# Keeping one block's outputs on chip instead of two, reading the last token rows behind the other block's scatter, and summing nine read pairs on TensorE over eight banks

## The chip, the cores and the metric

One core of one Trainium2 chip runs the whole program in one launch. The metric is the device time of an execution in microseconds (us). The kernel before takes 1036.44 us, the median of 3 runs (1035.94 to 1037.66).

## The reference

One layer of a hybrid backbone works on 640 tokens (128 prompt, 512 latent) of width 1024: a modulated norm, one input projection, a Fourier mixer and windowed attention, an output projection, then a mixture of experts and a last norm. The change lies in the mixture of experts and in the last norm behind it, and these lines say what they compute:

```python
idx, gates = route(xf, w_router, router_bias)          # 8 of 64 experts per token
...
def expert_block(args):
    tok, e = args
    xb = xpad[tok]
    hb = jax.nn.silu(xb @ w_gate[e]) * (xb @ w_up[e])
    return hb @ w_down[e]
rows = lax.map(expert_block, ...)
routed = jax.ops.segment_sum(rows.reshape(R, D) * row_gate[:, None], row_tok, ...)[:N]
shared = (jax.nn.silu(xf @ ws_gate) * (xf @ ws_up)) @ ws_down
...
x = x + gate * (routed + shared)
y = rms_norm(x, norm_f)
```

Everything is float32. Each token gets the gated outputs of eight experts summed; the eight are called its picks.

## The kernel before, in words

Tokens stand in five tiles of 128 (T = 5; tile 0 is the prompt). The routed rows are sorted into 49 blocks (NQ = 49, numbered 0 to 48) of four groups of 32 rows, each group with one expert. For each block GpSimd gathers 128 token rows, TensorE transposes them (`x_in`), multiplies with the gate and up weights (`block_gate_up`, 64 instructions), ScalarE and VectorE form silu(gate) * up (`silu`, `gated`), TensorE transposes that (`block_h`), and multiplies with the down weights (`block_down`, 32 instructions). ScalarE and VectorE scale half of the result each by the routing gate into `yb` (`y_half`, `y_out`), and GpSimd scatters the rows into a table in HBM, `expert_rows` (`y_dram`), by indirect DMA (line 791). Rows that hold no token are not written. The expert weights come through SP's queue into five homes (`ring` and a part of `reg_p`), 3 MB for an expert, each load issued when the home's former expert has been used.

The table has for each token tile eight picks of 128 rows. The picks of a token are sorted by expert. At the end SP reads the table back (line 706) in 20 requests of 1 MB, one for each token tile t and pair of picks j (`REQUESTS`, `PART = (6, 4, 2, 0)`: j = 0 are picks 6 and 7, j = 3 are picks 0 and 1). Request n goes into buffer n for the first 12, then buffers 5 to 11 are used again, each when its former content has been summed (`freed`). All go through one queue. The picks with high numbers can't come from the last experts, so request 0 needs block 44 scattered, and request 5 block 46.

The last two blocks, 47 (`KEPT`) and 48, are not scattered at all in the kernel before. Their rows in the table are set to zero early on (two indirect DMAs of zeros, line 824), and their outputs stay in `yb`. One-hot matrices `token_hit` (VectorE, `kept_tokens`) let TensorE add them to each tile's sum: out = token_hit x yb, two per block and tile (line 2320, line 2335 for the last tile). A read pair is summed in one of two ways: by VectorE with two additions of 128x1024 (`more_rows`, lines 1671 and 1672), or by TensorE with four products with the identity into the same banks (line 2327, line 2342). `PE_PAIRS` says which. j = 0 is always summed by VectorE within itself (`first_rows`, line 1666). `joined(t)` adds TensorE's sum to VectorE's, times the modulation gate, to the token tile `xs` (lines 1680, 1683, 1685), ScalarE then squares and roots (lines 1179, 1182), `finished(t)` scales by the norm (lines 1660, 1661), and SP writes the tile out (line 714). The last tile is done in two column halves (lines 1718, 1719, 1727; SP line 718). A float32 product of 128x512 stands in the trace as two MATMUL records.

## Time and profile before

| what | value |
|---|---|
| median of 3 runs | 1036.44 us |
| the profiled execution, its own time | 1036.7 us |
| its span in the trace | 1034.9 us |
| TensorE busy share of the span | 96% |
| VectorE | 33% |
| ScalarE, GpSimd | 22%, 16% |
| from HBM and to HBM | 298.76 MB, 31.39 MB |
| granted TensorE clock, mean | 0.992 |

The shares are means over stages with different limits. The blocks run from about 389 us to 985 us; the stage that the change rewrites is the last 70 us. A view with a time window shows which engine is full there and what another one waits for.

### The profile page before, as it was taken

The page shows a single profiled execution, that of the slowest core. Times are in us where ns is not written, and L with a number is a line of the kernel's source. Part 1 is how long each engine was busy: PE and PEld are TensorE (multiplying, and loading weights), DVE is VectorE, ACT ScalarE, POOL GpSimd, SP SyncE. Part 2 cuts the span into 40 slices and gives each one's busy share as a digit, 9 for nine tenths or more (in the row PEclk, how much of TensorE's full clock was granted, in tenths as well). Part 3 has the DMA queues.
Part 4 walks back from the last instruction along what each step waited for, and adds up shares of the span by engine and source line. Part 5 has one row for each costly group of instructions (what it writes and reads, how often), then busy time and mean ns, then how long its engine had stood idle before and what let it go on. Part 6 is the DMA issues. An engine that isn't in the chain of part 4 may idle for free.

```text
span 1034.9 us, 17713 instructions
## 1 busy us (share of the span) xinstructions
PE 997.8 (96%) x7069; PEld 445.8 (43%) x7069; DVE 338.3 (33%) x857; ACT 230.2 (22%) x549; POOL 161.9 (16%) x233
## 2 busy tenths in 40 slices
PE   6999999999999999999999999999999999999896
PEld 4435556565455553444333333333334433433242
DVE  1022225765136772322111111111112111112398
ACT  2131105665122240112111111111112111112111
POOL 1000010300131022111212211111211222111000
PEclk9999999999999999999999999999999999999998
DMA  9985408400101199999999999999999999999993
GB/s 326 384 333 192 163 32 226 201 2 1 62 21 41 48 387 388 398 421 420 419 422 421 417 420 380 400 421 419 419 419 419 414 372 399 419 420 420 419 409 139
DMA packets 64562, 321.60 MB, mean 311 GB/s; under 512 B 9768, under 2 KB 18624, under 8 KB 35040
## 3 DMA queue, kind: packets, MB, share of 16 engines
q1 hardware_dynamic: 48064, 272.71, 65.8%
q0 software_dynamic: 14240, 43.34, 10.6%
q10 hardware_dynamic: 2176, 4.41, 1.2%
q8 instruction: 57, 0.93, 0.4%
q14 instruction: 25, 0.20, 0.1%
HBM read 298.76 MB, written 31.39 MB: 319 GB/s over the span
## 4 chain that ended last, share of the span: by engine, by line
PE 83%; DMA 8%; DVE 5%; ACT 2%; issue 1%; SPq 1%; POOL 0%; DVEq 0%; POOLq 0%; ACTq 0%
PE bank L2211 30%; PE bank L2231 15%; PE bank L1973 7%; PE bank L1772 6%; DMA ring<-in_w_up 4%; PE bank L1756 4%; PE bank L2183 4%; PE bank L2067 3%; PE bank L2000 2%; PE bank L1986 2%; PE bank L1821 1%; PE bank L2073 1%; DMA ring<-expert_rows 1%; PE bank L1957 1%; DMA ring<-in_w_mod 1%
## 5 line engine op out<-in xcount | busy, mean ns | idle before, releaser
L2211 PE MATMUL bank<-ring,reg_h 128*32 128x512 f32 x2512 | 341.5, 598 | 5.3 <-DMA ring<-in_w_up 5.3
L2211 PEld LDWEIGHTS bank<-ring,reg_h 128*32 128x32 f32 x2512 | 102.4, 111 | 193.5 <-issue 193.3
L2231 PE MATMUL bank<-ring,reg_y 128*32 128x512 f32 x1256 | 174.1, 594 | 2.8 <-ACT reg_y L1109 2.0
L2211 PE MATMUL bank<-reg_p,reg_h 128*32 128x512 f32 x624 | 126.7, 592 | 0.0
L1597 DVE TENSOR_TENSOR reg_h<-reg_p,bank 128x256 f32<-128x256 f32 x49 | 20.6, 421 | 312.3 <-ACT reg_p L1127 282.1
L1127 ACT ACTIVATE reg_p<-bank 128x256 f32<-128x256 f32 x49 | 18.8, 384 | 309.0 <-PE bank L2211 309.0
L791 POOL DMA_INDIRECT expert_rows<-reg_y,rowc x47 | 47.3, 1007 | 239.3 <-DVE reg_y L1582 228.9
L2231 PEld LDWEIGHTS bank<-ring,reg_y 128*32 128x32 f32 x1256 | 48.0, 110 | 84.6 <-issue 79.6
L1582 DVE TENSOR_SCALAR reg_y<-bank,reg_p 128x512 f32<-128x512 f32 x49 | 36.8, 751 | 130.6 <-PE bank L2231 130.6
L1973 PE MATMUL bank<-ring,reg_h 128*128 128x512 f32 x160 | 70.3, 594 | 0.0
L1116 ACT ACTIVATE reg_y<-bank,reg_p 128x512 f32<-128x512 f32 x49 | 33.7, 688 | 151.0 <-PE bank L2231 147.3
L2231 PE MATMUL bank<-reg_p,reg_y 128*32 128x512 f32 x312 | 65.1, 593 | 0.0
L1772 PE MATMUL bank<-ring,reg_h 128*128 128x384 f32 (+2 forms) x192 | 63.2, 487 | 0.0
L777 POOL DMA_INDIRECT reg_h<-h_rows,tokc x49 | 51.3, 1047 | 39.2 <-POOL tokc L806 20.1
L2211 PEld LDWEIGHTS bank<-reg_p,reg_h 128*32 128x32 f32 x624 | 34.3, 110 | 42.6 <-issue 42.6
L2183 PE MATMUL bank<-keep,reg_h 128*128 128x128 f32 x392 | 48.5, 276 | 0.1
L2183 PEld LDWEIGHTS bank<-keep,reg_h 128*128 128x128 f32 x392 | 46.0, 192 | 2.8 <-issue 1.7
L1772 PEld LDWEIGHTS bank<-ring,reg_h 128*128 128x128 f32 x192 | 36.0, 190 | 25.7 <-issue 12.6
L1973 PEld LDWEIGHTS bank<-ring,reg_h 128*128 128x128 f32 x160 | 29.8, 190 | 34.6 <-issue 34.6
L1756 PE MATMUL bank<-ring,reg_h 128*128 128x512 f32 x96 | 43.0, 596 | 1.5 <-ACT reg_h L901 1.5
L1571 DVE COPY reg_h<-bank 128x512 f32<-128x512 f32 x49 | 33.9, 691 | 19.3 <-PE bank L2183 19.2
L1360 DVE CUSTOM_DVE_ANT_0 ring<-bank,reg_b,nsink 128x512 f32<-128x512 f32 (+2 forms) x60 | 34.5, 614 | 11.2 <-PE bank L1957 11.1
(304 smaller groups left out, 988.6 us busy)
## 6 DMA issues: line engine op xcount, KB each, us to landing
ring<-in_w_gate SPq DMA_DIRECT2D x51, 1024.0 KB, 13.2
ring<-in_w_up SPq DMA_DIRECT2D x51, 1024.0 KB, 19.9
ring<-in_w_down SPq DMA_DIRECT2D x51, 1024.0 KB, 17.5
ring<-in_w_mod SPq DMA_DIRECT2D x20, 1024.0 KB, 6.7
ring<-expert_rows SPq DMA_DIRECT2D x19, 1024.0 KB, 13.5
reg_p<-in_w_gate SPq DMA_DIRECT2D x13, 1024.0 KB, 16.6
reg_p<-in_w_up SPq DMA_DIRECT2D x13, 1024.0 KB, 21.8
reg_p<-in_w_down SPq DMA_DIRECT2D x13, 1024.0 KB, 19.8
```

The costliest lines, as they stand in the source:

```text
L777: pool.indirect_dma_start(out=xg[:, p, :], out_offset=None, in_=h2_dram, in_offset=bass.IndirectOffsetOnAxis(ap=tokc[:, p:p + 1], axis=0), ...
L791: pool.indirect_dma_start(out=y_dram, out_offset=bass.IndirectOffsetOnAxis(ap=rowc[:, p:p + 1], axis=0), in_=yb[:, p, :], in_offset=None, ...
L1116: act.activation(yb[:, p, 0:512], bank[source][:, :], ACT.Copy, scale=gate).then_inc(s_ya, 1)
L1360: dve.tensor_tensor_reduce(prob[:, p % 3, b, 0:nk], bank[2 * (p % 2) + b][:, 0:nk], masks[:, m0:m0 + len(keys), :].rearrange("p a b -> p ( ...
L1571: dve.tensor_copy(xg_t[:, p, 512:1024], source[:, :]).then_inc(s_xb, 1)
L1582: dve.tensor_scalar(yb[:, p, 512:1024], bank[source][:, :], gate, None, ALU.mult).then_inc(s_yb, 1)
L1756: last = pe.matmul(bank[2 + 3 * t + g][:, :], h1t[:, k, t * P:(t + 1) * P], w[:, 512 * g:512 * g + 512], start=(k == 0), stop=(k == KD - 1))
L1772: last = pe.matmul(bank[4 + g % 2][:, 0:WIDTHS[g]], h1t[:, k, t * P:(t + 1) * P], win_part(k, g), start=(k == 0), stop=(k == KD - 1))
L1973: last = pe.matmul(bank[2 * (t % 2) + hf][:, :], mix_t[:, k, t * P:(t + 1) * P], w, start=(k == 0), stop=(k == KD - 1))
L2183: last = pe.transpose(bank[banks[k // 4]][:, (k % 4) * P:(k % 4 + 1) * P], v[:, k, :], ident)
L2211: last = pe.matmul(bank[2 + p][R * j:R * j + R, :], xg_t[:, p, k * P + R * j:k * P + R * j + R], w_gu(homes[n % SLOTS])[:, k], start=(k == ...
L2231: last = pe.matmul(bank[y_banks(b)[hf]][R * j:R * j + R, :], h_t[:, p, i * P + R * j:i * P + R * j + R], w_dn(homes[n % SLOTS])[:, i, 512 ...
```

## The change

Block 47's outputs are no longer kept. GpSimd scatters them behind all the other scatters (a new indirect DMA with its own row numbers `rowk`), and only block 48 keeps zeros in the table, one-hots and products. Requests 10 to 19 hold all picks 0 to 3 and wait for that scatter. To have block 47's outputs early, its down product is put between the two halves of block 48's gate and up products, and ScalarE writes both halves of them. The order of reads changes from tile by tile to all j = 0, all j = 1, then j = 2 and 3 tile by tile. TensorE sums nine pairs instead of seven, each of the first four tiles in two banks of its own, and VectorE sums six instead of eight.

```diff
-        PE_PAIRS = ((3,), (3,), (3,), (2, 3), (2, 3))
+        PE_PAIRS = ((3,), (2, 3), (2, 3), (2, 3), (2, 3))
-            return t if j == 0 else ACC + 3 * t + j - 1
+            return t + ACC * j if j < 2 else 2 * ACC + 2 * t + j - 2
...
-            sp.wait_ge(s_zero, 32)
+            sp.wait_ge(s_zero, 16)
             for n, (t, j) in enumerate(REQUESTS):
...
+                if n == 2 * ACC:
+                    sp.wait_ge(s_zero, 32)
...
-            for p in range(2):
-                pool.indirect_dma_start(out=y_dram, out_offset=bass.IndirectOffsetOnAxis(ap=rowc[:, p:p + 1], axis=0),
-                                        in_=zeros, in_offset=None,
-                                        bounds_check=NROW - 1, oob_is_err=False).then_inc(s_zero, 16)
+            pool.indirect_dma_start(out=y_dram, out_offset=bass.IndirectOffsetOnAxis(ap=rowc[:, 0:1], axis=0),
+                                    in_=zeros, in_offset=None,
+                                    bounds_check=NROW - 1, oob_is_err=False).then_inc(s_zero, 16)
...
+            pool.wait_ge(s_ya, KEPT + 1)
+            pool.wait_ge(s_yb, KEPT + 1)
+            pool.indirect_dma_start(out=y_dram, out_offset=bass.IndirectOffsetOnAxis(ap=rowk[:, 0:1], axis=0),
+                                    in_=yb[:, KEPT % 2, :], in_offset=None,
+                                    bounds_check=NROW - 1, oob_is_err=False).then_inc(s_zero, 16)
...
             silu(KEPT, 1)
-            silu(KEPT + 1, 0)
             h_t_out(KEPT, 1)
             y_half(KEPT, 1, extra * 16 + scattered(KEPT), gate_s[:, KEPT:KEPT + 1], y_banks(KEPT)[0])
+            act.activation(yb[:, 1, 512:1024], bank[y_banks(KEPT)[1]][:, :], ACT.Copy, scale=gate_s[:, KEPT:KEPT + 1]).then_inc(s_yb, 1)
+            silu(KEPT + 1, 0)
...
             block_gate_up(KEPT)
-            block_gate_up(KEPT + 1)
+            block_gate_up(KEPT + 1, range(KD // 2))
             block_h(KEPT, 1)
             block_down(KEPT)
+            block_gate_up(KEPT + 1, range(KD // 2, KD))
             block_h(KEPT + 1, 0)
             block_down(KEPT + 1)
...
-            for t in range(T - 2):
+            gated(KEPT, 1)
+            for t in range(4):
                 first_rows(t)
-            gated(KEPT, 1)
-            first_rows(T - 2)
             gated(KEPT + 1, 0)
-            first_rows(T - 1)
-            y_half(KEPT, 1, extra * 16 + scattered(KEPT), gate_s[:, KEPT:KEPT + 1], y_banks(KEPT)[1])
+            first_rows(4)
             more_rows(0, 1)
             y_out(KEPT + 1)
+            for t in range(1, T):
+                more_rows(t, 1)
             more_rows(0, 2)
...
```

On TensorE, at the head of the tail in the kernel before, behind block 48's down product (line 2320 adds kept rows with one-hots in `reg_b`, line 2327 adds read rows in `ring`; a row is one product, which the trace shows as two records):

```order
L2320 MATMUL bank0<-reg_y,reg_b 128x512
L2320 MATMUL bank1<-reg_y,reg_b 128x512
...
L2327 MATMUL bank0<-ring,keep 128x512
L2327 MATMUL bank1<-ring,keep 128x512
...
L2320 MATMUL bank2<-reg_y,reg_b 128x512
L2320 MATMUL bank3<-reg_y,reg_b 128x512
...
L2327 MATMUL bank2<-ring,keep 128x512
L2327 MATMUL bank3<-ring,keep 128x512
```

And in the changed kernel at the same place (its lines 2318 and 2326 are those of 2320 and 2327 before):

```order
L2318 MATMUL bank0<-reg_y,reg_b 128x512
L2318 MATMUL bank1<-reg_y,reg_b 128x512
L2318 MATMUL bank2<-reg_y,reg_b 128x512
L2318 MATMUL bank3<-reg_y,reg_b 128x512
L2318 MATMUL bank4<-reg_y,reg_b 128x512
L2318 MATMUL bank5<-reg_y,reg_b 128x512
L2318 MATMUL bank6<-reg_y,reg_b 128x512
L2318 MATMUL bank7<-reg_y,reg_b 128x512
L2326 MATMUL bank0<-ring,keep 128x512
L2326 MATMUL bank1<-ring,keep 128x512
```

Before, each tile had four products with kept rows and then four or eight with read rows, over banks 0 to 3 in turn. Now eight products with kept rows of four tiles stand first, 28 with read rows of those tiles follow with nothing between them, and the last tile has one kept and four read products for each of its two halves.

On TensorE, where blocks 47 and 48 are multiplied, before (line 2211 gate and up, 2073 transposes, 2231 down; bank3 is block 47's, bank2 block 48's):

```order
L2211 MATMUL bank3<-ring,reg_h 32x512 x32
L2211 MATMUL bank2<-ring,reg_h 32x512
L2211 MATMUL bank2<-reg_p,reg_h 32x512 x3
...
L2073 MATMUL bank4<-keep,reg_h 128x128 x2
L2231 MATMUL bank0<-ring,reg_y 32x512 x8
```

And in the changed kernel (lines 2213, 2074, 2234):

```order
L2213 MATMUL bank2<-reg_p,reg_h 32x512 x3
L2074 MATMUL bank4<-keep,reg_h 128x128 x2
L2234 MATMUL bank0<-ring,reg_y 32x512 x8
L2234 MATMUL bank1<-ring,reg_y 32x512 x8
L2213 MATMUL bank2<-ring,reg_h 32x512
```

Block 47's transposes and its down product moved ahead of half of block 48's gate and up products.

On SP, the reads of the table before, the last rows of the queue (the names in brackets are the semaphores that a read waits for):

```order
L706 DMA ring<-expert_rows 128x2048 [waits block_gate_up_done] x4
L706 DMA ring<-expert_rows 128x2048 [waits block_down_done] x2
L706 DMA ring<-expert_rows 128x2048 [waits second_rows_summed_by_dve] x2
L706 DMA ring<-expert_rows 128x2048 [waits token_rows_summed_by_pe]
```

And in the changed kernel:

```order
L710 DMA ring<-expert_rows 128x2048 [waits block_gate_up_done] x4
L710 DMA ring<-expert_rows 128x2048 [waits block_down_done,zero_rows_then_last_but_one_block_out]
L710 DMA ring<-expert_rows 128x2048 [waits block_down_done]
L710 DMA ring<-expert_rows 128x2048 [waits second_rows_summed_by_dve] x6
L710 DMA ring<-expert_rows 128x2048 [waits token_rows_summed_by_pe]
```

Request 10, the second of these rows, now waits for the scatter of block 47, and six reads instead of five wait for VectorE's sums.

## Rows read from the trace of the kernel before

**Rows 1.** The page: busy time of an engine; DMA share in 40 slices of the span

```profile
PE 997.8 (96%) x7069; PEld 445.8 (43%) x7069; DVE 338.3 (33%) x857; ACT 230.2 (22%) x549; POOL 161.9 (16%) x233
...
DMA  9985408400101199999999999999999999999993
```

**Rows 2.** The chain that ended last, from 930 us: start, us, what

```profile
1025.76 1.28 DVE xs L1661
...
1028.37 0.61 DVE reg_h L1718
```

**Rows 3.** Timeline of TensorE in the tail: start, us, instruction, count, [idle before]

```profile
985.14 3.70 PE L2320 MATMUL bank<-reg_y,reg_b 128*128 128x512 f32 x8
...
1009.28 7.03 PE L2327 MATMUL bank<-ring,keep 128*128 128x512 f32 x16
1016.14 1.88 PE L2335 MATMUL bank<-reg_y,reg_b 128*128 128x512 f32 x4
...
1023.01 3.60 PE L2342 MATMUL bank<-ring,keep 128*128 128x512 f32 x8
```

**Rows 4.** Timeline of VectorE and SP's queue in the tail

```profile
988.89 1.23 DVE L1671 TENSOR_TENSOR ring<-ring 128x1024 f32<-128x1024 f32 x1 [0.42 <-DMA ring<-expert_rows]
...
993.93 1.28 DVE L1680 TENSOR_TENSOR ring<-ring,bank 128x512 f32<-128x512 f32 x2
...
997.65 1.22 DVE L1671 TENSOR_TENSOR ring<-ring 128x1024 f32<-128x1024 f32 x1
...
1016.10 0.34 SPq L714 DMA_DIRECT2D out_y_prompt<-xs  x1
```

**Rows 5.** Timeline of all engines around blocks 47 and 48

```profile
960.57 0.75 DVE L1582 TENSOR_SCALAR reg_y<-bank,reg_p 128x512 f32<-128x512 f32 x1 [3.73 <-PE bank L2231]
962.17 0.97 POOL L791 DMA_INDIRECT expert_rows<-reg_y,rowc  x1 [4.52 <-DVE reg_y L1582]
...
967.43 0.38 ACT L1127 ACTIVATE reg_p<-bank 128x256 f32<-128x256 f32 x1 [6.18 <-PE bank L2211]
...
968.82 1.23 DVE L1666 TENSOR_TENSOR ring<-ring 128x1024 f32<-128x1024 f32 x1 [7.50 <-DMA ring<-expert_rows]
...
975.75 0.51 PE L2073 MATMUL bank<-keep,reg_h 128*128 128x128 f32 x2 [1.51 <-DVE reg_h L1597]
...
980.57 0.69 ACT L1116 ACTIVATE reg_y<-bank,reg_p 128x512 f32<-128x512 f32 x1 [3.90 <-PE bank L2231]
```

**Rows 6.** SP's queue, 969 to 972 us, and all DMAs on the table, issue to landing

```profile
970.12 2.18 SPq L706 DMA_DIRECT2D ring<-expert_rows  x3
...
DMA to landing us min/median/max: 8.2/10.3/20.1
```

**Rows 7.** GpSimd's zero scatters, and DMA queues from 414.9 to 422 us

```profile
410.55 0.99 POOL L824 DMA_INDIRECT expert_rows<-reg_b,rowc  x1 [0.30 <-issue]
...
q0 software_dynamic: 272, 0.62, 22.2%
```

**Rows 8.** Timeline of TensorE at its two waits for weights

```profile
530.45 5.77 PE L2211 MATMUL bank<-ring,reg_h 128*32 128x512 f32 x36 [2.06 <-DMA ring<-in_w_up]
...
674.81 5.43 PE L2211 MATMUL bank<-ring,reg_h 128*32 128x512 f32 x36 [3.25 <-DMA ring<-in_w_up]
```

**Rows 9.** Stretches: us, busy us (instructions) by engine, granted clock, DMA share, GB/s

```profile
530.84:534.24 3.40, 3.40 (x20) 1.08 (x16) 0.00 (x0) 0.00 (x0) 0.23 (x1) 0.50 1.02 425
534.25:540.00 5.75, 5.75 (x55) 2.41 (x48) 0.30 (x1) 0.69 (x2) 0.00 (x0) 1.00 1.01 422
674.20:677.60 3.40, 2.79 (x16) 0.92 (x20) 0.00 (x0) 0.00 (x0) 0.05 (x1) 0.50 1.00 418
677.70:682.00 4.30, 4.30 (x44) 1.36 (x40) 0.00 (x0) 0.00 (x0) 0.00 (x0) 1.00 1.02 424
...
985.14:1026.61 41.47, 41.47 (x100) 18.15 (x96) 39.93 (x41) 7.75 (x14) 0.00 (x0) 1.00 0.72 296
```

**Rows 10.** A stretch while the weights stream, columns as above

```profile
600.00:640.00 40.00, 40.00 (x368) 16.05 (x364) 7.84 (x19) 7.54 (x15) 8.78 (x15) 1.00 0.96 395
```

More of the change, by code:

```diff
@@ L1602, in kept_tokens @@
             def kept_tokens():
-                dve.wait_ge(s_zero, 32)
-                for i in range(2):
-                    kept = slice(KEPT + i, KEPT + i + 1)
-                    for t in range(T):
-                        last = dve.tensor_scalar(token_at[:, i, t:t + 1], tok_i[:, kept], float(-t * P), None, ALU.add)
+                dve.wait_ge(s_zero, 16)
+                for t in range(T):
+                    last = dve.tensor_scalar(token_at[:, t:t + 1], tok_i[:, KEPT + 1:KEPT + 2], float(-t * P), None, ALU.add)
                 link(last)
-                for i in range(2):
-                    for t in range(T):
-                        last = dve.tensor_scalar(token_hit[i][:, t, :], iota, token_at[:, i, t:t + 1], None, ALU.is_equal)
+                for t in range(T):
+                    last = dve.tensor_scalar(token_hit[:, t, :], iota, token_at[:, t:t + 1], None, ALU.is_equal)
                 last.then_inc(s_kept, 1)
@@ L1679, in joined @@
                     cols = slice(512 * hf, 512 * hf + 512)
-                    last = dve.tensor_tensor(half[:, cols], half[:, cols], bank[2 * (t % 2) + hf][:, :], ALU.add)
+                    last = dve.tensor_tensor(half[:, cols], half[:, cols], bank[2 * t + hf][:, :], ALU.add)
                 last.then_inc(s_tq, 1)
@@ L1713, in _ @@
             link(dve.tensor_tensor(xs[:, t, :], xs[:, t, :], ahead, ALU.add))
+            joined(1)
+            finished(0)
+            joined(2)
+            finished(1)
+            joined(3)
+            finished(2)
             finished(T - 2)
@@ L2309, in _ @@
             pe.wait_ge(s_kept, 1)
-            pe.wait_ge(s_ya, KEPT + 1)
-            pe.wait_ge(s_yb, KEPT + 1)
+            pe.wait_ge(s_ya, NQ)
+            pe.wait_ge(s_yb, NQ)
             for t in range(T - 1):
-                if t >= 2:
-                    pe.wait_ge(s_tq, t - 1)
-                for i, p in ((0, 1), (1, 0)):
-                    if t == 0 and i:
-                        pe.wait_ge(s_ya, NQ)
-                        pe.wait_ge(s_yb, NQ)
-                    for hf in range(2):
-                        pe.matmul(bank[2 * (t % 2) + hf][:, :], token_hit[i][:, t, :], yb[:, p, 512 * hf:512 * hf + 512],
-                                  start=(i == 0), stop=False)
+                for hf in range(2):
+                    pe.matmul(bank[2 * t + hf][:, :], token_hit[:, t, :], yb[:, (KEPT + 1) % 2, 512 * hf:512 * hf + 512],
+                              start=True, stop=False)
+            for t in range(T - 1):
                 for j in PE_PAIRS[t]:
```

59 lines of the change are left out of this document (25 added, 34 removed).

## The prediction

> **What bounds the kernel now.** I read the page first, then the chain of waits of the last 100 us, then the timeline there engine by engine, and then stretches of it. The page says that TensorE is busy 96% of the span and that the DMA engines are full from slice 17 on, with a thin last slice [rows 1]. So two things are full at once in the expert stage, and it takes the rows to see which one ends last where.
>
> In the tail the chain runs over VectorE: from the addition at 988.89 us, over the scaling at 1025.76, to the last half's product at 1028.37 nearly every link is a VectorE instruction [rows 2, 4]. The reader should see that this is close. From 985.14 to 1026.61 us TensorE is busy for all of 41.47 us and VectorE for 39.93 us [rows 9]. TensorE's rows follow each other without idle time: 16 records from 1009.28 to 1016.14, that is 0.429 us each, and 0.858 us for a product of two [rows 3]. It ends at 1023.01 + 3.60 = 1026.61, and VectorE comes to the last half's bank only at 1028.37 [rows 2, 3].
>
> The third player is the stream of reads. The ninth read (request 8) releases VectorE at 988.89; the last one releases SP's first output at 1016.10 [rows 4]. That is 11 reads in 27.21 us, 2.47 us for a read of 1 MB. All before them were queued as closely. So the k-th read lands at 988.89 + 2.47 (k - 9), and the twelfth (request 11) at 996.3. Before the change this pace hurts nobody, since VectorE and TensorE both get work from the reads in step.
>
> **The change part by part.**
>
> *Fewer products and additions.* TensorE had 5 x 4 products with kept rows and 7 x 4 with reads, 48 in all. It gets 5 x 2 and 9 x 4, 46: 1.7 us less work. VectorE loses two pairs, each two additions of 1.25 us (988.89 to 997.65 holds four of these and the joining of tile 0; the joining takes 997.65 - 993.93 = 3.72), so 5.0 us of work less [rows 4]. If work were all, the tail would be shorter.
>
> *The new order of reads.* Requests 0 to 10 are now all VectorE's, and 11 to 19 are all TensorE's. TensorE's products with kept rows can start when block 48's output is there. After that it has nothing until request 11 lands. Where is it by then? Block 48's gate and up products start when block 47's silu starts, at 967.43 [rows 5], and take 6.9 us; the first half ends at 970.85. Block 47's transposes follow at once, because `gated` now stands ahead of `first_rows` on VectorE; before, they waited until 975.75 [rows 5]. From transposes to the scaled output it takes 980.57 - 975.75 = 4.8 us [rows 5], so ScalarE starts on block 47's output at 975.7 and, with two activations of 0.69 us [rows 5], is through at 977.1. Block 48's second half runs 975.3 to 978.7, its silu and `gated` take about 1.1 us, and its output is ready at 979.8 + 4.8 + 0.7 = 985.3. That is where the kernel before started its products with kept rows (985.14 [rows 3]), so nothing is lost or won. Eight products take 6.9 us: TensorE runs dry at 992.2.
>
> *The scatter of block 47.* Between the end of the scaling (961.32) and the issue (962.17) there were 0.85 us before [rows 5], so it is issued at about 977.9. The last scatter before was issued at 962.17 and let SP go on at 970.12, 7.95 us later; over all DMAs on this table the figures are 8.2, 10.3 and 20.1 us [rows 5, 6]. So it lands at about 986 (985.9 to 998). Request 10 waits for it. But the reads ahead of it last until 991.4 in the pace above, so SP's wait is covered by what is queued: the read has to be issued some 1.4 us before the queue runs empty. The cover is gone if the scatter takes over 13 us. Behind request 10 in SP's queue stand the other nine reads; their buffers are free in time (VectorE ends a pair each 2.5 us from 984 on). The scatter's own bytes do cost: at most 128 rows of 4 KB, 0.52 MB or 1.24 us at 422 GB/s [rows 9]; the two zero scatters of blocks 47 and 48 are most of 0.62 MB on the software queue, so 0.31 MB or 0.73 us each if equal [rows 7]. I take **+1.0 us** on every later read (0.73 to 1.24). Request 11 then lands at 997.3.
>
> *TensorE behind it.* From there on TensorE needs 0.858 x 4 = 3.43 us for a pair and a pair lands each 2.47 us, so it is never short again, and never has a pause either. Seven pairs, then one kept product and two pairs in two halves: 28 + 2 + 8 = 38 products, 32.6 us. With 0.3 us to start it ends at 1030.2, and VectorE comes to the last half at 1030.4 instead of 1028.37: **+2.0 us**. VectorE is not later than that by itself: tile 3 can be joined at 997.6 + 7 x 3.43 = 1021.6, then 3.7 for joining, twice 1.5 for the scaling of tiles 2 and 3 (an instruction of 1.28 [rows 2] behind a reciprocal), and 1.4 for the first half: 1029.7, 0.7 us ahead. What follows it to the end is unchanged.
>
> *The clock.* TensorE stands still from 992.2 to 997.6, 5.4 us. In the trace a pause of 2.06 us is followed by a stretch with a granted clock of 0.50 (1.2 instead of 2.4 GHz), and so is one of 3.25 us [rows 8, 9], while the pause of 1.51 us at 975.75 isn't [rows 5, 9]. The new pause is longer than both, so I expect one such stretch. Its price: 20 instructions in 3.40 us where 55 in 5.75 us is the pace after it (12.5 instructions or 1.3 us lost), and 16 in 2.79 us against 44 in 4.30 us (1.2 us lost) [rows 9]; halved throughout it would be 1.7. For these dense products I take **+1.5 us**, with 0 and two stretches, 3.0, as bounds.
>
> *The zero scatter that goes.* It saves GpSimd 0.99 us, hidden, and the DMA engines its bytes, 0.73 to 1.24 us, at a place from which they are full (share 1.01 at 422 GB/s) [rows 7, 9]. TensorE waits twice for weights, 2.06 and 3.25 us [rows 8]. Both landings move forward: **-1.0 us** for everything after 674.81. More is possible: a pause of 1.06 us may leave the clock up at 530.84 and save another 1.3 us, which lasts only if the loads around 600 to 640, where DMA is not quite full (0.96), follow TensorE [rows 9, 10]. Less too, if homes and not bytes set these landings. Bounds 0 and -2.3. The shorter one-hot work on VectorE is beside block products and costs or gives nothing.
>
> *Sum.* 1036.7 (the profiled execution) - 1.0 + 2.0 + 1.5 = 1039.2. The median of the runs is 0.3 us below that execution, so 1038.9.
>
> **The rivals.**
>
> *Smaller than can be told.* The same tail, with the weights' landings 2.3 us earlier: 1036.4 - 2.3 + 2.0 + 1.5 = 1037.6. Or with no low clock: 1036.4 - 1.0 + 2.0 = 1037.4. For it: half of the terms are single pauses. Against it: the pause is 5.4 us.
>
> *Faster: VectorE was the bound and is relieved.* If TensorE were never without reads, its 46 products would run from 985.3 to 1024.8 and VectorE would come to the last half at 1025.0, 3.4 us earlier; with the zero scatter's 1.0 us that is 1032.0. The chain of waits speaks for it, as it names VectorE at almost every step [rows 2]. It decides from the point where request 11 lands by 992.2; the pace of the reads puts that 5 us later, and no part of the change moves bytes away from before it.
>
> *Slower still: a late scatter.* If block 47's scatter lands later than about 991, each further us is a us at the end. With the longest, 20.1 us, it lands at 998, the end moves by 7 us to 1045.9. The scatter before was issued while VectorE had nothing to do for 7.50 us; the new one falls among additions of 1.23 us with both inputs in SBUF [rows 5]. Four of them in its way would be 5 us, and it would land at 991, at the edge. The Trainium skill, page "SBUF — State Buffer", section "Who interferes with whom", has such a rule: a VectorE instruction with two SBUF inputs contends with a GpSimd instruction that reads SBUF. By that rule the scatter's issue is held up by VectorE; no row of this trace shows a scatter beside such additions, so it is open here.
>
> **How the numbers follow.** The forecast (pause on TensorE, low clock, weights about 1 us earlier) 0.56; smaller than can be told 0.28; relieved and faster 0.06; late scatter 0.06; something else 0.04, split. 0.2% is 2.07 us, about what a measurement of this kernel can tell from no change. The forecast itself goes from 1038.0 to 1040.7, and a part of it lies within 0.2%: slower 0.58, same 0.34, faster 0.08. The range has to take in the smaller cases, down to 1036.6 (all of -2.3 and no full stretch of low clock), and up to 1041.0 (no gain from the weights, more than one stretch).
>
> **What would show it.** In the changed kernel's timeline TensorE has, behind the kept products (line 2318), a pause of about 5 us that a DMA on `expert_rows` ends at about 997, then 76 records without a gap, and a stretch with clock 0.50 at or just behind the pause. VectorE, full before, has idle time in front of `joined` (line 1687), ended by TensorE. SP's request 10 is issued at about 986 and the reads keep their 2.47 us. The last halves (line 1719) wait for TensorE. The pause at 530 is about 1 us. I am wrong if TensorE's first read pair starts before 994, if the reads' stream has a hole behind the scatter, or if the end waits for VectorE.

## The result, and the profile after

The changed kernel takes 1041.83 us, the median of 8 runs (1039.36 to 1044.12), against 1036.19 us for the kernel before (8 runs, 1033.97 to 1039.55). The ratio is 1.0048, with a 95% interval of 1.0032 to 1.0064: 5 us slower. That is the direction of the forecast, but above its 1038.9 us and above the upper end of its range, 1041.0.

The page of the changed kernel answers to [rows 1]. TensorE is as busy as before, VectorE has 6.6 us less work, and the DMA line is nearly the same.

```profile
PE 998.0 (96%) x7065; PEld 445.6 (43%) x7065; DVE 331.7 (32%) x842; ACT 230.9 (22%) x550; POOL 162.5 (16%) x233
...
DMA  9994409300110199999999999999999999999993
```

The chain that ended last no longer runs over VectorE, as it did in [rows 2]. From 970 us on it is (start, us, what):

```profile
975.91 9.95 DMA expert_rows<-reg_y,rowk
...
985.88 0.32 SPq L710
...
986.24 9.53 DMA ring<-expert_rows
...
995.81 26.50 PE bank L2326 x56
1022.31 0.86 PE bank L2333 x2
1023.17 3.43 PE bank L2340 x8
1026.61 0.86 PE bank L2333 x2
1027.46 3.45 PE bank L2340 x8
...
1030.93 0.70 DVE reg_h L1719
```

Read it from the bottom: the last half of the last tile waits for TensorE, TensorE has worked without a break since 995.81, it started there because a read of the table landed, and the chain goes on through SP's queue to the scatter of block 47. The timelines of TensorE and VectorE show the same from their side:

```profile
983.71 7.11 PE L2318 MATMUL bank<-reg_y,reg_b 128*128 128x512 f32 x16 [1.07 <-DVE reg_y L1592]
995.81 26.50 PE L2326 MATMUL bank<-ring,keep 128*128 128x512 f32 x56 [5.00 <-DMA ring<-expert_rows]
...
1001.82 1.28 DVE L1687 TENSOR_TENSOR ring<-ring,bank 128x512 f32<-128x512 f32 x2 [5.64 <-PE bank L2326]
...
1030.93 0.69 DVE L1719 TENSOR_TENSOR reg_h<-bank,reg_b 128x512 f32<-128x512 f32 x1 [0.43 <-PE bank L2340]
```

Both engines stand still, TensorE for 5.00 us and VectorE for 5.64. Three stretches (columns as in [rows 9]) add the clock:

```profile
983.71:995.81 12.10, 7.11 (x16) 2.93 (x16) 11.64 (x10) 0.00 (x0) 0.00 (x0) 0.90 0.90 359
995.81:1000.28 4.47, 4.47 (x6) 1.89 (x7) 0.37 (x1) 0.00 (x0) 0.00 (x0) 0.50 1.02 429
1000.28:1030.90 30.62, 30.62 (x72) 13.29 (x70) 24.11 (x28) 7.42 (x14) 0.00 (x0) 1.00 0.58 236
```

Behind the pause the granted clock is 0.50 for 4.47 us, in which 6 records get done; at full clock each takes 0.43 us. The clock had already fallen inside the pause:

```profile
993.45:1000.28 6.83, 4.47 (x6) 1.89 (x7) 2.66 (x3) 0.00 (x0) 0.00 (x0) 0.50 1.02 428
```

The half clock lasts 6.83 us, and TensorE works for 4.47 of them. The read that it waits for lands 9.53 us behind its request, and from 1000.28 on the DMA share is only 0.58: all reads are early except the one that TensorE starts with.

**A fixed point to measure from.** Executions differ in their first 76 to 79 us, so two traces are compared by the distance to a fixed point P, the start of the eight small transposes that follow TensorE's wait of 0.94 us there (line 1788; line 1787 before). In the changed kernel:

```profile
76.22 1.06 PE L1788 MATMUL bank<-keep,ring 128*128 128x128 f32 x8 [0.94 <-DVE ring L1269]
```

In the kernel before the row starts at 78.10. From P to the end of the span it is 1034.9 - 78.10 = 956.8 us before and 1037.5 - 76.22 = 961.3 after: 4.5 us. The medians differ by 5.6 us, the own times of the two profiled executions only by 2.7 (1039.36 - 1036.7), since that of the changed kernel is the shortest of its eight and has its P 1.9 us earlier. P moves with the clock at the very start. From 14 to 18 us (first the kernel before, then the changed one):

```profile
14.00:18.00 4.00, 3.04 (x16) 0.68 (x16) 0.00 (x0) 0.00 (x0) 0.00 (x0) 0.68 1.01 391
14.00:18.00 4.00, 3.40 (x28) 1.81 (x29) 0.88 (x2) 0.00 (x0) 0.00 (x0) 1.00 1.02 387
```

Over all 17 traces of this document, the nine whose P is at 77.78 us or later have a clock of 0.83 from 10 to 20 us, and the eight whose P is at 76.95 or earlier have 1.00, whichever kernel it is.

### The profile page after: what moved, and what is told of

It is laid out like the page before. It is cut to its first block, busy times and chain, and to the rows that moved or that the text cites. A ratio compares the mean times of both kernels' runs of the same rounds, so it can differ in the third digit from the quotient of the medians.

```text
span 1037.5 us, 17689 instructions
## 1 busy us (share of the span) xinstructions
PE 998.0 (96%) x7065; PEld 445.6 (43%) x7065; DVE 331.7 (32%) x842; ACT 230.9 (22%) x550; POOL 162.5 (16%) x233
## 4 chain that ended last, share of the span: by engine, by line
PE 87%; DMA 7%; DVE 2%; ACT 1%; issue 1%; SPq 1%; DVEq 0%; POOLq 0%; ACTq 0%
PE bank L2213 30%; PE bank L2234 15%; PE bank L1974 7%; PE bank L1773 6%; DMA ring<-in_w_up 4%; PE bank L1757 4%; PE bank L2184 4%; PE bank L2068 3%; PE bank L2326 3%; PE bank L2001 2%; PE bank L2081 2%; PE bank L2074 2%; PE bank L1987 2%; PE bank L1822 1%; PE bank L1958 1%
## 5 line engine op out<-in xcount | busy, mean ns | idle before, releaser
L795 POOL DMA_INDIRECT expert_rows<-reg_y,rowc x47 | 47.4, 1010 | 239.1 <-DVE reg_y L1592 237.7
L781 POOL DMA_INDIRECT reg_h<-h_rows,tokc x49 | 51.2, 1045 | 39.0 <-POOL tokc L810 20.8
```

Of the source, the lines that this page charges most:

```text
L781: pool.indirect_dma_start(out=xg[:, p, :], out_offset=None, in_=h2_dram, in_offset=bass.IndirectOffsetOnAxis(ap=tokc[:, p:p + 1], axis=0), ...
L795: pool.indirect_dma_start(out=y_dram, out_offset=bass.IndirectOffsetOnAxis(ap=rowc[:, p:p + 1], axis=0), in_=yb[:, p, :], in_offset=None, ...
```

## The experiments

Each was timed beside the kernel before on the same chip, and "before" is the median of that kernel there. "P to end" is from each one's profile, a single execution. Theory A is that of the prediction (standstill, half clock, and reads that come late for TensorE), theory B a late scatter.

| run | us, median | before, beside it | ratio, 95% interval | P | P to end |
|---|---|---|---|---|---|
| (before, profiled) | | | | 78.10 | 956.8 |
| again: the changed kernel | 1041.9 | 1037.4 | 1.0045 (1.0029 to 1.0061) | 76.95 | 962.6 |
| fill | 1039.66 | 1037.4 | 1.0020 (1.0006 to 1.0033) | 76.75 | 959.6 |
| noscatter | 1039.5 | 1037.4 | 1.0019 (1.0002 to 1.0036) | 78.24 | 959.3 |
| fed | 1039.46 | 1037.4 | 1.0013 (0.9997 to 1.0030) | 78.83 | 958.2 |
| split | 1035.91 | 1036.87 | 0.9991 (0.9978 to 1.0003) | 77.78 | 955.7 |
| twozero | 1040.19 | 1036.87 | 1.0034 (1.0019 to 1.0049) | 76.45 | 960.6 |
| relief | 1036.25 | 1036.87 | 0.9998 (0.9983 to 1.0012) | 76.56 | 957.8 |
| offload | 1039.34 | 1036.87 | 1.0028 (1.0014 to 1.0042) | 78.15 | 960.0 |
| fillns | 1038.07 | 1036.27 | 1.0021 (1.0009 to 1.0034) | 76.52 | 958.9 |
| join | 1035.9 | 1036.27 | 1.0002 (0.9987 to 1.0017) | 77.79 | 957.2 |
| splitjoin | 1036.07 | 1036.27 | 0.9996 (0.9983 to 1.0009) | 76.57 | 955.7 |
| warm | 1034.09 | 1036.27 | 0.9981 (0.9968 to 0.9993) | 76.41 | 955.2 |
| warmb | 1037.17 | 1036.9 | 1.0000 (0.9989 to 1.0011) | 77.89 | 958.6 |
| warma | 1039.32 | 1036.9 | 1.0039 (1.0024 to 1.0054) | 78.17 | 959.2 |
| warm2 | 1034.13 | 1036.9 | 0.9975 (0.9964 to 0.9985) | 78.62 | 955.1 |

**again**, the changed kernel without an edit.

> The changed kernel once more, unchanged, for another trace and the clock of each run. Theory A (TensorE is left without reads and then loses clock): a pause of 4.5 to 5.5 us ahead of the first read product, at least 3.4 us of half clock behind it, about 5 us slower than before, and runs with a lower mean clock take longer. Theory B (the scatter of block 47 lands late in most executions and holds the reads): the slower the run, the longer from the scatter's issue to its landing, with a hole in the DMA stream, and no relation to the clock.

It repeats the loss. TensorE and the clock in its trace:

```profile
985.57 7.10 PE L2318 MATMUL bank<-reg_y,reg_b 128*128 128x512 f32 x16 [1.03 <-DVE reg_y L1592]
997.06 7.48 PE L2326 MATMUL bank<-ring,keep 128*128 128x512 f32 x10 [4.38 <-DMA ring<-expert_rows]
```

```profile
997.06:1002.98 5.92, 5.92 (x7) 2.53 (x8) 0.84 (x1) 0.00 (x0) 0.00 (x0) 0.50 1.00 418
```

The pause is shorter than in the first trace (4.38 against 5.00 us), and more of TensorE's work falls under the low clock (5.92 against 4.47 us). Theory B fails on its own sign: from the scatter's issue to SP's next read it is 8.45 us here and 9.95 in the first trace, and this execution is the longer one (1041.33 against 1039.36 us). Theory A's last sign holds only roughly: the shortest four of the twelve runs have mean clocks of 0.992 and 0.993 and the longest four 0.990 to 0.991, but the longest of all, 1045.35 us, has 0.991.

**fill**: products on data at hand in the pause.

```diff
+            for i in range(5):
+                pe.matmul(bank[i][:, :], token_hit[:, 0, :], yb[:, (KEPT + 1) % 2, 0:512], start=True, stop=True)
             for t in range(T - 1):
                 for hf in range(2):
```

> Five kept products more are computed ahead of the real ones, into banks that are started anew afterwards, so that TensorE works through most of its pause (4.3 us); nothing of the result changes. Theory A: the pause falls from 5.0 to under 1.5 us, no half clock in the tail, and the time falls by the clock's part, 1.5 to 3 us against the changed kernel; the first read product starts when it did. Theory B: no change, within 1 us.

```profile
985.60 4.53 PE L2317 MATMUL bank<-reg_y,reg_b 128*128 128x512 f32 x10 [1.03 <-DVE reg_y L1592]
989.96 7.03 PE L2320 MATMUL bank<-reg_y,reg_b 128*128 128x512 f32 x16
996.83 3.60 PE L2328 MATMUL bank<-ring,keep 128*128 128x512 f32 x8
```

```profile
996.83:1029.65 32.82, 32.78 (x77) 14.25 (x75) 25.21 (x30) 7.45 (x14) 0.00 (x0) 1.00 0.67 278
```

No pause, no low clock, and 32.82 us from the first read product to the last half, where it was 1030.93 - 995.81 = 35.12 us in the changed kernel and 1032.91 - 997.06 = 35.85 in its repeat. The difference, 2.3 and 3.0 us, is the price of the low clock by itself. The median falls by 2.2 us, as theory A had it. What stays, 0.2%, is something else.

**noscatter**: block 47's rows get zeros early, and its scatter goes.

```diff
...
-            pool.wait_ge(s_ya, KEPT + 1)
-            pool.wait_ge(s_yb, KEPT + 1)
-            pool.indirect_dma_start(out=y_dram, out_offset=bass.IndirectOffsetOnAxis(ap=rowk[:, 0:1], axis=0),
-                                    in_=yb[:, KEPT % 2, :], in_offset=None,
-                                    bounds_check=NROW - 1, oob_is_err=False).then_inc(s_zero, 16)
...
```

> Block 47 is not scattered at all and its rows in the table are zeroed as in the kernel before, so its outputs are missing from the result; no read waits for it. Theory A: reads land about 1 us earlier (the scatter's bytes), the pause and the half clock stay, 0.5 to 1.5 us faster than the changed kernel. Theory B: most of the loss is gone, 3 us or more faster than the changed kernel.

```profile
996.22 4.25 PE L2323 MATMUL bank<-ring,keep 128*128 128x512 f32 x6 [2.81 <-DMA ring<-expert_rows]
```

The read that TensorE waits for lands at 996.22 - 78.24 = 918.0 us from P. With the scatter it was 919.6 (changed kernel) and 920.1 (repeat). So the scatter costs the reads behind it 1.6 to 2.1 us by these single traces (1.5 against twozero, which has as many zero scatters as noscatter); it does not cost several. Even without it TensorE pauses for 2.81 us and the clock falls (34.62 us instead of 32.82 to the last half, 1.8 us). The median is 2.4 us below that of the changed kernel, between what theory A gave (0.5 to 1.5) and what theory B gave (3 or more). So the scatter matters more than theory A had it, by medians about half of the 4.5 us above before, since a read that lands later also lengthens the pause. It is not all of the loss, and its landing is no later in the longer execution (again).

Its bytes are only a part of it. From its issue to SP's next read the software queue moves 0.39 MB, in the changed kernel, its repeat and twozero alike, which is 0.9 us at 422 GB/s [rows 9]. The rest may be that the stream of reads is not full while SP waits. In the changed kernel:

```profile
984.00:986.00 2.00, 2.00 (x6) 0.82 (x5) 1.92 (x2) 0.00 (x0) 0.00 (x0) 1.00 0.68 287
986.00:988.00 2.00, 2.00 (x6) 0.89 (x5) 1.83 (x2) 0.00 (x0) 0.00 (x0) 1.00 0.69 168
```

SP goes on at 985.88. The same 2 us have 0.90 in the repeat, 0.81 in twozero and 0.76 in warma. But noscatter has such a stretch too, 0.74 from 980 to 982 us, so that the scatter causes it is not shown.

**fillns**, both edits at once.

> The changed kernel with both edits of earlier runs at once: five products on data at hand ahead of TensorE's kept products, so that it does not stand still, and no scatter of block 47 (its rows are zero in the table, so the output lacks block 47). What is left of the change is the order of reads and who sums what. If pause, clock and scatter are separate prices, the time is that of the kernel with the fill less what the scatter costs the reads: theory A puts that at 1 to 2 us, so the whole comes within 1 us of the kernel before. Theory B (the scatter's landing is most of the loss) expects the same or less. If the order of reads has a price of its own, the time stays 1.5 us or more above before.

It stays 0.2%, 1.8 us by medians, above before and tells less than hoped: the five products and the kept ones behind them last until 995.95, or 919.4 us from P, so they hid the 1.4 us that the reads had gained. From P to the end it is 0.7 us shorter than the kernel with the fill.

**fed**: TensorE's pairs chosen so that early reads feed it.

```diff
-        PE_PAIRS = ((3,), (2, 3), (2, 3), (2, 3), (2, 3))
...
+        PE_PAIRS = ((3,), (3,), (1, 2, 3), (1, 2, 3), (2, 3))
+        PE_ORDER = ((2, 1), (3, 1), (0, 3), (1, 3), (2, 2), (2, 3), (3, 2), (3, 3))
...
```

> TensorE also sums pair 1 of tiles 2 and 3, whose reads are there when the kept products end, ahead of its first late pair, and VectorE sums pair 2 of tile 1 instead of them: ten pairs against five. Theory A: no pause over 1 us, no half clock, TensorE ends about 4 us earlier than in the changed kernel and the time is within 1.5 us of the kernel before (4 to 5 us faster than the changed one). Theory B: the late scatter still holds the reads, at most 2 us faster than the changed kernel.

TensorE has no pause and full clock from 986.94 to 1030.40 (43.42 of 43.46 us busy), and from P the last half starts 3.1 and 4.4 us earlier than in the two traces of the changed kernel. Yet the median falls by only 2.4 us, where theory A had 4 to 5, and stays 2.1 above before. What lasts is the number of products: 50 of 0.858 us behind one another are 42.9 us, and the last half waits for TensorE. VectorE stands still for reads (4.97 and 2.45 us), so it is not the bound. The rest of the miss is not traced.

**split**: the kernel before with block 47's down product between the halves of block 48's gate and up products (the lines are those of the change), nothing else.

> The kernel before with one part of the change alone: block 47's down product between the two halves of block 48's gate and up products, both halves of its output written by ScalarE, its gated product first on VectorE; both blocks are still kept, and the requests, pairs and banks are those of before. Theory A (the loss of the change comes from TensorE's standstill, its half clock and the order of reads in the tail): the time is that of before within 0.5 us, since block 48's output is ready at the same point (TensorE's products with kept rows begin within 0.5 us of where they did), and the reads of the tail begin as before. Rival: the split has a price of its own, because block 48's gate and up products end some 2.7 us later (977.0 against 974.3), and the reads that wait for the homes they free are issued later; then VectorE's additions in the tail start later and the end moves by 1 us or more.

No price that can be told. From P to the end it is 1.1 us shorter than before, the median is 1.0 us lower, and the interval holds no change.

**twozero**: the changed kernel with the zero scatter that it had dropped.

```diff
...
+            pool.indirect_dma_start(out=y_dram, out_offset=bass.IndirectOffsetOnAxis(ap=rowk[:, 0:1], axis=0),
+                                    in_=zeros, in_offset=None,
+                                    bounds_check=NROW - 1, oob_is_err=False).then_inc(s_zero, 16)
...
```

> The changed kernel with the zero scatter of block 47's rows put back beside that of block 48 (block 47's real scatter stays). It tests the term of -1.0 us that the prediction gave to the zero scatter that goes. If the prediction's term is right, the weights that TensorE waits for at about 528 and 672 us land 0.7 to 1.2 us later, and the whole is 1.0 us longer than the changed kernel. Rival, from the three runs so far in which that landing stood no earlier against a fixed point than before: no difference beyond the measurement (under 0.5 us).

```profile
672.58 7.70 PE L2216 MATMUL bank<-ring,reg_h 128*32 128x512 f32 x44 [5.08 <-DMA ring<-in_w_up]
```

The weights land at 672.58 - 76.45 = 596.1 us from P with two zero scatters. With one they landed at 596.7 (672.96 - 76.22, changed kernel) and 597.1 (674.00 - 76.95, repeat), and in the kernel before, with two, at 674.81 - 78.10 = 596.7. No gain from the one that goes; the time is 0.1% lower with it put back, within the intervals.

The traces say where the bytes went. The same 5 us, from 347 us behind P on, in the kernel before, the changed kernel and twozero:

```profile
425.10:430.10 5.00, 5.00 (x52) 1.82 (x48) 0.75 (x1) 0.69 (x1) 2.30 (x4) 1.00 1.00 402
423.22:428.22 5.00, 5.00 (x52) 1.75 (x47) 0.75 (x1) 0.69 (x1) 2.00 (x4) 1.00 0.88 306
423.45:428.45 5.00, 5.00 (x52) 1.89 (x48) 0.66 (x1) 0.64 (x1) 1.99 (x4) 1.00 0.99 339
```

At the start of these stretches SP has waited 6.6 us until a down product of TensorE has freed a home, and issues the next load of weights at 347.2, 347.1 and 346.9 us from P. With one zero scatter the DMA engines are through with the loads before it earlier and stand idle until it begins: 0.12 of 5 us, 0.6 us, nearly the 0.73 that the prediction took as the scatter's least. The share is lowest right behind the issue, 0.54 from 425 to 426 us. All five traces with one zero scatter have 0.88 to 0.90 there, all twelve with two 0.97 to 1.01.

**relief**: two of VectorE's additions on 8 of 1024 columns.

```diff
-                link(dve.tensor_tensor(half, half, rows[:, 0, :], ALU.add))
...
+                n = 8 if (t, j) == (0, 2) else D
+                link(dve.tensor_tensor(half[:, 0:n], half[:, 0:n], rows[:, 0, 0:n], ALU.add))
...
```

> The kernel before with VectorE's two additions of the third pair of tile 0 done on 8 of 1024 columns (the output lacks the rest of these sums): 2.5 us less work for VectorE in the tail, nothing else changed. It measures how much VectorE, on which the chain of the kernel before ends, could give back at most before TensorE is the bound. By the rows of before TensorE ends at 1026.6 and VectorE came to the last half at 1028.4, so the time falls by 1.5 to 1.8 us and TensorE ends the chain. Rival: the additions had cover (VectorE would wait for the reads instead), and the time stays within 0.5 us.

Taking 2.5 us of work off the engine that the chain of before names at every step gives nothing that can be told. In this trace TensorE waited 2.27 us for block 47's gated product, which stands behind VectorE's first additions, had a stretch of half clock behind it, and started its kept rows at 986.21 (909.7 us from P against 907.0 before):

```profile
975.12 0.51 PE L2074 MATMUL bank<-keep,reg_h 128*128 128x128 f32 x2 [2.27 <-DVE reg_h L1597]
```

So the trace shows one way in which the gain is lost. That it is the way in the other runs is not shown.

**offload**: the last scaling of four tiles moved from VectorE to GpSimd and ScalarE.

```diff
...
-                dve.scalar_tensor_tensor(xs[:, t, :], xs[:, t, :], rstd[:, r], nfbc, ALU.mult, ALU.mult).then_inc(s_fin, 1)
+                dve.reciprocal(rstd[:, r], rstd[:, r]).then_inc(s_cexp, 1)
...
+                pool.tensor_tensor(token_rows(t)[:, 1, :], xs[:, t, :], nfbc, ALU.mult).then_inc(s_clr, 1)
...
```

> The kernel before with the last scaling of tiles 0 to 3 taken from VectorE: GpSimd multiplies the token tile with the norm's weights, ScalarE scales it by the root's reciprocal, and VectorE only forms that reciprocal (5.1 us less work for VectorE in the tail). If the engines do not disturb each other, VectorE is relieved and TensorE ends the chain: the time falls by 1.5 to 1.8 us, as in the run without two additions. Rival: GpSimd's multiplications with both inputs in SBUF and VectorE's additions with both inputs in SBUF hold each other up; four multiplications of some 2.4 us then stand in VectorE's way, and the time is 1 to 4 us longer than before. The row to look at is the duration of VectorE's additions that stand beside a multiplication of GpSimd (1.23 us alone).

```profile
998.33 3.16 POOL L860 TENSOR_TENSOR ring<-xs,reg_b 128x1024 f32<-128x1024 f32 x1 [34.22 <-DVE xs L1691]
999.31 3.25 DVE L1678 TENSOR_TENSOR ring<-ring 128x1024 f32<-128x1024 f32 x1
```

The rival holds: an addition of 1.23 us takes 3.25 us when a multiplication of GpSimd is under way, four times over (3.25 or 3.26 us each), and the time rises by 0.28%, 2.5 us by medians.

**join**: the last tile's sum handed to TensorE; and **splitjoin**, the same on top of split.

```diff
...
-            link(dve.tensor_tensor(ahead, ahead, g2bc[:, 1, :], ALU.mult))
-            link(dve.tensor_tensor(xs[:, t, :], xs[:, t, :], ahead, ALU.add))
...
+                    if j == 3:
+                        pe.wait_ge(s_du, DVE_PAIRS.index((t, 1)) + 1)
+                        pe.matmul(bank[2 * (t % 2) + hf][:, :], ident, token_rows(t)[:, 0, cols], start=False, stop=False)
...
```

> The kernel before, with VectorE's sum of the last tile handed to TensorE: two products with the identity (0.86 us) in place of VectorE's multiplication and addition of 128x1024 (2.4 us), whose work the last halves now do with the rest. No read, scatter or block is touched. From rows of before TensorE ends at 1026.6 + 0.86 = 1027.5 and VectorE's own work reaches the last half at 1028.4 - 2.5 = 1025.9, so the last half starts at 1027.7 instead of 1028.3: 0.6 to 0.7 us less, which is too little to tell from no change in the whole. In the trace the last halves wait for TensorE. Rival: nothing is gained at all, as in the run without two additions, because TensorE itself starts later whenever VectorE's first additions stand ahead of block 47's gated product.

> The kernel before with two edits: block 47's down product between the halves of block 48's gate and up products (the run of that part alone), and the last tile's sum handed to TensorE. The first frees TensorE's start from VectorE's additions, the second takes 2.5 us of VectorE's work away for 0.86 us of TensorE's. In the run with the first alone, TensorE's products began at 983.35 and would end at 1024.8, and VectorE came to the last half at 1026.9. With both, TensorE ends at 1025.7 and the last half starts at 1025.9: 1.0 us less than with the split alone, and 1.5 to 2 us less than before. Rival: within 0.5 us of the split alone.

Neither can be told from before. In splitjoin VectorE is free early, but the scaling of tile 3 then waits for ScalarE's root:

```profile
1022.92 0.16 DVE L1661 RECIPROCAL rstd<-rstd 128x1 f32<-128x1 f32 x1 [1.54 <-ACT rstd L1183]
```

So 1.54 of the 2.4 us saved turn into a new wait; the 1.0 us expected over split did not come, and the rival (within 0.5 us) is right.

**warm**: splitjoin with products on data at hand ahead of TensorE's two waits for weights.

```diff
...
+                    for i in range({11: 2, 23: 4}.get(b, 0)):
+                        pe.matmul(bank[2 + p][:, :], ident, xg_t[:, p, 0:512], start=True, stop=True)
                     for n in sorted(set(tiles)):
                         if FIRST[n] >= 4 * b:
                             pe.wait_ge(*gate_up_in(n))
...
```

> The kernel with both edits (split and join), and with two and four products on data at hand ahead of TensorE's two waits for weights (blocks 11 and 23), so that it does not stand still there. If the half clock behind these waits is a price that lasts to the end, 1 to 1.3 us for each that vanishes: 1 to 2.5 us less than split and join alone. Rival: the clock stays up but the time stays, within 0.5 us, because the weights' stream and not TensorE sets the next 100 us; or the four products are longer than the wait and cost a part of a us.

```profile
20.00:1029.90 1009.90, 989.55 (x7011) 437.37 (x7011) 329.22 (x836) 224.14 (x538) 157.52 (x220) 1.00 0.78 312
```

The granted clock is 1.00 over 1010 us, and the median is 2.2 us below before and 2.0 below splitjoin, as expected. **warm2** repeats it:

> The kernel with split, join and the products at the waits for weights once more, unchanged, to see whether its 2 us under the kernel before hold: a ratio of 0.998 to 0.9985. Rival: nothing is left of it, within 0.05% of before.

2.8 us below before, ratio 0.9975. This version beats both kernels.

**warmb**, the same products in the kernel before, nothing else.

> The kernel before with nothing but the two and four products on data at hand ahead of TensorE's waits for weights in blocks 11 and 23; its tail is untouched. If the half clock behind these waits is a price that lasts to the end, the time falls by 1.5 to 2.5 us and the granted clock is 1.00 from 10 us to the last stretch. Rival: the gain of the kernel with three edits needs the two in the tail as well, and this one stays within 0.5 us of before.

Its rival is right: no gain at all. The trace of VectorE and TensorE says where it went:

```profile
973.63 1.23 DVE L1666 TENSOR_TENSOR ring<-ring 128x1024 f32<-128x1024 f32 x1 [1.26 <-DMA ring<-expert_rows]
974.89 0.42 DVE L1597 TENSOR_TENSOR reg_h<-reg_p,bank 128x256 f32<-128x256 f32 x1
```

```profile
975.37 0.70 PE L2073 MATMUL bank<-keep,reg_h 128*128 128x128 f32 x2 [3.20 <-DVE reg_h L1597]
```

```profile
974.21:981.03 6.82, 5.20 (x26) 1.51 (x30) 3.94 (x5) 0.37 (x1) 0.00 (x0) 0.50 1.01 425
```

TensorE comes to the tail 1.9 us earlier (block 46's down product starts at 954.80, 876.9 us from P, instead of 956.86, 878.8), but block 47's gated product stands on VectorE behind three additions whose reads land when they always did. It starts at 974.89, 897.0 us from P, against 897.2 before. TensorE's wait there grows from 1.51 [rows 5] to 3.20 us, and the clock falls behind it. In warm the gated product stands first, as in split, and the gain lasts. Split, join, the two together and the products alone give nothing that can be told; all three together give 2 to 3 us. Whether join has a part in it is not shown, since no run has split and the products without it.

**warma**, the same products in the changed kernel with the fill.

> The changed kernel with the five products ahead of its kept rows and the two and four products ahead of the waits for weights: no stretch of half clock is left between 10 us and the end. If half clock is what stands between the changed kernel and before beyond the order of reads, this gains 1.5 to 2.5 us on the run with the five products alone (2 us above before) and comes to within 1 us of the kernel before. Rival: it stays at 2 us above before, which would put that loss on the tail.

Again the rival. TensorE's first read lands at 997.87 - 78.17 = 919.7 us from P, where it was before the edit:

```profile
997.87 2.41 PE L2330 MATMUL bank<-ring,keep 128*128 128x512 f32 x5 [1.33 <-DMA ring<-expert_rows]
```

The changed kernel's chain is the stream of reads up to this one and then 32.8 us of TensorE. An earlier TensorE just waits for it longer. The median is 2.4 us above before; the ratio, 1.0039, says 4 us, because four of the twelve runs took 1042 to 1045 us. What these four have is not shown.

## Why the prediction was right, and where it was wrong

**The mechanism in the tail was right.** TensorE is dry behind the kept products, is released by request 11, is never short again, and VectorE comes to the last half behind it. The chain of waits and fill bear it out, and split shows that the new order of blocks 47 and 48 is not what costs.

**When request 11 lands (+2.0): right, in part by luck.** The prediction had TensorE start on it at 997.6 - 78.10 = 919.5 us from P; measured were 919.6 and 920.1 (919.5 in twozero, 919.7 in warma). Within that, the scatter's share was set too small: 1.0 us predicted, 1.6 to 2.1 measured. The reads ahead of it were set 0.5 us too late (a start at 996.6 - 78.10 = 918.5 without the scatter, against the 918.0 of noscatter), and the two nearly cancel. SP issued request 10 at 985.88, which looks like the forecast's 986 and is not: from P it is 909.7 us for 907.9. The wait was not all covered by queued reads either: the DMA share was 0.68 and 0.69 around that time in the changed kernel, a thin place where the prediction had named a hole as a sign of being wrong. The pause was 5.00 and 4.38 us for 5.4 forecast.

**The clock (+1.5): right in kind, too small in size.** The term was one stretch of 3.40 us, as in the block stage. In the tail of the changed kernel and of its repeat the half clock lasted 6.83 us, with 4.47 and 5.92 us of TensorE's work in it, and cost 2.3 and 3.0 us. That is the prediction's upper bound of two stretches, 3.0, and not the value that it took.

**The zero scatter that goes (-1.0): wrong.** This step failed. "Both landings move forward" rested on the DMA engines being full from that place on. From P, the weights landed at 452.5 and 596.7 us (changed kernel) against 452.4 and 596.7 before:

```profile
672.96 7.27 PE L2213 MATMUL bank<-ring,reg_h 128*32 128x512 f32 x52 [3.16 <-DMA ring<-in_w_up]
```

In all five traces with one zero scatter the second landing stood at 596.7 to 597.6, in the twelve with two at 595.3 to 596.7. Dropping it brought nothing, and twozero did not lose by its return. The engines were full, but not with work that was free to move forward: SP issues the next weights when TensorE has freed a home, at 347 us from P with one zero scatter or two, and the time saved before stands there as idle time of the DMA engines (share 0.88 instead of 1.00, under twozero). The prediction had this as a doubt, "if homes and not bytes set these landings", and gave it the bound 0. Its sign, a pause of about 1 us at 530, did not come: 2.24 and 2.58 us.

**The sum.** Without the -1.0 and with 2.3 to 3.0 for the clock, the working gives 1036.4 + 2.0 + 2.3 to 3.0 = 1040.7 to 1041.4, with 0.1 to 0.6 us more for a later landing; 1041.83 was measured. The traces close better. From P the last half starts at 919.6 + 32.8 = 952.4 us plus 2.3 for the clock, against 1028.28 - 78.10 = 950.2 before: 2.2 + 2.3 = 4.5 us, and in the repeat 2.8 + 3.0 = 5.8. These are the differences in "P to end", so nothing is left for a gain from the weights. The upper end of the range was 0.8 us short: 1041.0 is 1036.4 + 2.0 + 2.6, less than no gain from the weights and two stretches of half clock give together (1041.4).

**The rivals.** "VectorE was the bound and is relieved" had the chain of before on its side, and relief shows how little was in it. "Smaller than can be told" needed the weights 2.3 us earlier or no low clock, and neither came. "A late scatter" fell: the longest time from issue to SP's next read in the changed kernel's two traces was 9.95 us, not 13. Yet an addition in the scatter's way is real (last section).

**What makes the change lose** stands in the prediction: the kernel before has TensorE's kept products strewn among the reads; the change puts them first and lets 38 products, 32.6 us by its count and 32.8 measured, follow one read whose landing the DMA stream sets.

## What to carry to other kernels

Where two engines and a stream end within 2 us of each other, taking work from one can give nothing while waits tie them. Here the gated product ahead of the additions, the last sum on TensorE and work at hand for the standstill were worth nothing alone, and 2 to 3 us together. A chain of waits that names one engine at every step does not say how much that engine could give back; compare where the next one ends. Cost a pause of TensorE as the pause and the clock behind it, and take the clock from several stretches, with the longest as its bound. Before bytes saved on a full DMA stream count as time, look whether a later transfer waits for something that does not move.

## What the runs showed of the hardware

**The scatter's issue is held by an addition.** In fill, the repeat and twozero the issue of block 47's scatter, with no addition under way, took 0.97, 0.96 and 0.96 us. In the changed kernel it took 1.52, in fed 1.86 and in warma 1.31 us, each time with an addition of VectorE under way (the changed kernel, then fed):

```profile
975.37 1.23 DVE L1673 TENSOR_TENSOR ring<-ring 128x1024 f32<-128x1024 f32 x1 [1.27 <-DMA ring<-expert_rows]
975.91 1.52 POOL L860 DMA_INDIRECT expert_rows<-reg_y,rowk  x1 [14.52 <-ACT reg_y L1182]
```

```profile
978.60 1.22 DVE L1673 TENSOR_TENSOR ring<-ring 128x1024 f32<-128x1024 f32 x1 [1.26 <-DMA ring<-expert_rows]
978.80 1.86 POOL L860 DMA_INDIRECT expert_rows<-reg_y,rowk  x1 [14.52 <-ACT reg_y L1182]
```

The addition ends at 976.60 and 979.82 (977.85 in warma), and the issue 0.83, 0.84 and 0.84 us later: as if it began about when the addition was through. In these three it pays a part of one addition, not the four that the prediction feared. In offload the like shows between two computing instructions, and there the addition, which comes second each time, takes 2.0 us longer. The Trainium skill, page "SBUF — State Buffer", section "Who interferes with whom", says that a VectorE instruction with two SBUF inputs contends with a GpSimd instruction that reads SBUF, and calls the ports that they share an exclusive lock. The rows of offload agree, with 3.25 for 1.23 us. The same section of the Trainium skill infers that a `tensor_tensor` does not hold up the generation of a DMA's descriptors. The issues of 1.31 to 1.86 us do not fit that for this scatter, and the measurement decides; which part of the issue waits is not shown.

**A pause does not fix what the clock does.** TensorE's waits for weights of 2.06 us (before), 2.24 (changed kernel) and 2.23 (relief) were followed by half clock, but those of 2.58 us in the repeat, 2.10 in offload and even 3.52 in fed were not:

```profile
676.38:682.60 6.22, 6.21 (x60) 2.36 (x64) 0.00 (x0) 0.00 (x0) 0.00 (x0) 1.00 1.01 421
```

In the tail the half clock lasted 6.83 us with the pauses of 5.00 and 4.38 us, and 3.41 us with the 4.23 of twozero. It began inside the pause each time, so the work under it differs too: 4.47, 5.92 and 3.14 us. In twozero:

```profile
995.92:999.06 3.14, 3.14 (x4) 1.51 (x5) 0.99 (x1) 0.00 (x0) 0.00 (x0) 0.50 1.01 428
```

The price at the end was 2.3, 3.0 and, in twozero (34.46 us to the last half for 32.82), 1.6 us.
